# Weight chunks of the projections: eight buffers of two times 128 rows instead of four of four times 128

## The reference, cut to what matters

```python
# first block
h = rms_norm(x, norm1_g) @ w_in            # 2048 x 6176: q, k, v, gates (32 columns), ...
x = x + concat([gla(h), dilated_attention(h)]) @ w_out      # 2048 x 2048
x = x + peer_ffn(rms_norm(x, norm2_g))     # gathers rows of two tables of 16384 x 2048
# second block
p = rms_norm_2(x, mix_norm_g) @ w_in_2     # lru, mlstm (8 gate columns), moba inputs
x = x + concat([lru(p), mlstm(p), moba(p)]) @ w_out_2       # 2048 x 2048
x = x + memory_cross_attention(rms_norm_2(x, xa_norm_g), rms_norm_2(mem, mem_norm_g), wq, wkv, wo)
return rms_norm_2(x, final_norm_g)
```

## Time and profile before

| what | value |
|---|---|
| median of 3 runs | 2442.86 us |
| the profiled execution: its own time | 2440.96 us |
| its span in the trace | 2439.2 us |
| PE busy | 2017.3 us, 83% |
| DVE busy | 1354.1 us, 56% |
| ACT busy | 623.8 us, 26% |
| POOL busy | 630.3 us, 26% |
| mean granted TensorE clock | 0.948 |

### The profile page before, as it was taken

The page is one execution under the profiler, slowest core; times in us unless marked ns, Lnnn a source line. Parts: engine busy times, 40 slices in busy tenths (PEclk is TensorE's granted clock), DMA queues, the critical chain, the costliest instruction groups (busy, mean ns, idle before and its releaser), DMA issues. The chain is left out here.

```text
span 2439.2 us, 21677 instructions
## 1 busy us (share of the span) xinstructions
PE 2017.3 (83%) x8013; PEld 1331.2 (55%) x8013; DVE 1354.1 (56%) x1820; ACT 623.8 (26%) x901; POOL 630.3 (26%) x523
## 2 busy tenths in 40 slices
PE   6999867984988989777777888898771899999975
PEld 5888746873444444322233434443220888999874
DVE  4446537447554556455555654665547755555444
ACT  4334325321011111111111111011001554354333
POOL 0000000006543544445355434444533000000000
PEclk9999958996999999999999999999996899999988
DMA  5555501729999999999999999999998544465531
GB/s 197 197 195 190 199 1 47 264 85 382 421 422 422 422 421 422 423 421 419 421 422 420 416 422 421 416 420 423 421 422 343 180 160 158 146 205 186 188 122 70
DMA packets 102203, 727.64 MB, mean 298 GB/s; under 512 B 11840, under 2 KB 11968, under 8 KB 19808
## 3 DMA queue, kind: packets, MB, share of 16 engines
q0 software_dynamic: 73728, 536.90, 53.1%
q1 hardware_dynamic: 28384, 189.52, 22.0%
HBM read 722.18 MB, written 4.19 MB: 298 GB/s over the span
## 5 line engine op out<-in xcount | busy, mean ns | idle before, releaser
L1248 PE MATMUL bank<-ring,work 128*128 128x512 f32 x1920 | 894.0, 609 | 240.1 <-DMA ring<-in_peer_up_dram,work 238.7
L1492 DVE CUSTOM_DVE_ANT_0 ring<-ring,mix_t 128x2048 f32<-128x2048 f32 x256 | 584.2, 2291 | 526.7 <-DMA ring<-in_peer_down_dram,work 526.5
L1248 PEld LDWEIGHTS bank<-ring,work 128*128 128x128 f32 x1920 | 350.5, 192 | 716.5 <-issue 504.3
L449 DVE TENSOR_TENSOR ring_r<-ring,ring_r 128x2048 fp32r<-128x2048 f32 (+2 forms) x150 | 320.0, 2136 | 319.4 <-ACT ring_r L428 319.0
L1376 POOL DMA_INDIRECT ring<-in_peer_down_dram,work x256 | 316.6, 1237 | 440.1 <-DVE work L1449 238.2
L1385 POOL DMA_INDIRECT ring<-in_peer_up_dram,work x240 | 284.4, 1185 | 480.4 <-PE bank L1248 421.6
L482 PE MATMUL bank<-ring_r,mix_r 128*128 128x512 f32 (+1 forms) x1248 | 393.2, 386 | 0.0
L428 ACT ACTIVATE ring_r<-ring 128x2048 fp32r<-128x2048 f32 (+2 forms) x150 | 267.6, 1787 | 307.1 <-DMA ring<-in_w_out_dram 90.4
L482 PE MATMUL bank<-ring_r,act_r 128*128 128x512 f32 (+1 forms) x864 | 309.4, 388 | 12.6 <-DVE ring_r L449 12.6
L1316 ACT ACTIVATE work<-const,work 128x128 f32<-128x128 f32 x240 | 91.5, 399 | 734.3 <-PE bank L1248 733.1
L482 PEld LDWEIGHTS bank<-ring_r,mix_r 128*128 128x128 f32 x1248 | 233.6, 188 | 43.5
(11 more groups left out here) (354 smaller groups left out, 1336.3 us busy)
## 6 DMA issues: line engine op xcount, KB each, us to landing
ring<-in_w_out_dram SPq DMA_DIRECT2D x32, 1024.0 KB, 4.8
ring<-in_w_in_qk_dram SPq DMA_DIRECT2D x24, 1024.0 KB, 4.8
ring<-in_w_in_rest_dram SPq DMA_DIRECT2D x24, 1024.0 KB, 4.8
ring<-in_w_in_mo_dram SPq DMA_DIRECT2D x24, 768.0 KB, 4.4
h<-in_w_query_dram SPq DMA_DIRECT2D x8, 2048.0 KB, 10.4
ring<-in_w_in_ml_oz_dram SPq DMA_DIRECT2D x12, 1024.0 KB, 4.8
h<-in_xa_wkv_dram SPq DMA_DIRECT2D x4, 2048.0 KB, 16.8
ring<-in_w_in_lru_dram SPq DMA_DIRECT2D x8, 1024.0 KB, 4.9
```

What stands on the lines that cost most here:

```text
L449: dve.tensor_tensor(low(c), raw(c), plain(high(c)), ALU.subtract).then_inc(k.weights_low, 1)
L1248: m = pe.matmul(B[c][:, :], diag[:, j % DEPTH, :], up_row(j)[:, c * 512:(c + 1) * 512], start=first, stop=last)
L1492: dve.tensor_tensor_reduce(down_row(j), down_row(j), xn[:, t, :], 1.0, 0.0, ALU.mult, ALU.add, dots[:, p, j:j + 1]).then_inc(down_used, 1)
```

## The change

`DEEP` = 2 sets how many times 128 rows a chunk has; there are 16 / DEEP = 8 slots of half the size over the same memory, so the ring holds the same bytes. The two gate jobs take 8 times 128 rows, in two chunks each. A tick stays what it was in work: `PER_TICK` = 2 chunks. `AHEAD` stays at 3 ticks, which are now 6 chunks; the work beside the projections, the activation splits and the take-outs keep their places relative to the weights.

```diff
@@ class Program
+        self.pieces = shaped(self.ring[:, :], 2 * SLOTS, DEEP * 512)
+        self.pieces_r = shaped(self.ring_r[:, :], 2 * SLOTS, DEEP * 512)
@@
-SLOTS = 4
-AHEAD = SLOTS - 1
+DEEP = 2
+SLOTS = 16 // DEEP
+PER_TICK = 4 // DEEP
+AHEAD = 3
@@ class Job
-    def __init__(self, w, kind, dest, act, m=P, keep=None, add=False, deep=4):
+    def __init__(self, w, kind, dest, act, m=P, keep=None, add=False, deep=None):
-        self.deep, self.chunks = deep, KC // deep
+        self.deep = deep or DEEP
+        self.chunks = KC // self.deep
@@ def project
     def high(c):
-        return k.slots_r[:, SLOTS + c.slot, 0:c.job.deep * c.job.cols]
+        return k.pieces_r[:, SLOTS + c.slot, 0:c.job.deep * c.job.cols]
     def parts_at(p):
-        per_chunk = chunks[0].job.deep // 4
+        per_chunk = max(1, chunks[0].job.deep // 4)
+        if chunks[0].job.deep < 4:
+            return range(p // PER_TICK, p // PER_TICK + 1) if p % PER_TICK == 0 and p // PER_TICK < len(splits) else range(0)
         return range(len(splits))[p * per_chunk:(p + 1) * per_chunk]
     def taken_at(p):
-        return [chunks[p - AHEAD]] if 0 <= p - AHEAD < len(chunks) and chunks[p - AHEAD].completing else []
+        last = p - AHEAD * PER_TICK + PER_TICK - 1
+        return [chunks[last]] if 0 <= last < len(chunks) and chunks[last].completing else []
+    def at_tick(at, p):
+        if p % PER_TICK == 0:
+            at(p // PER_TICK)
@@ SP, ACT, DVE and PE programs
-                at(p - AHEAD)
+                at_tick(at, p - AHEAD * PER_TICK)
-                at(p)
+                at_tick(at, p)
@@ def build, def second_block
-        gates_job = Job(..., whole_act, m=GATE_M, keep=32, deep=KC)
+        gates_job = Job(..., from_act, m=GATE_M, keep=32, deep=KC // 2)
-            stream.chunks[stream.at(out2, e, s)].needs = needs
+            stream.chunks[stream.at(out2, e, s * PER_TICK)].needs = needs
```

More of the change, by code:

```diff
@@ L230, in __init__ @@
         self.groups = self.cols // m if kind == "feat" else NT
-        self.deep, self.chunks = deep, KC // deep
+        self.deep = deep or DEEP
+        self.chunks = KC // self.deep
         self.add_waits = ()
         if kind == "fold":
-            self.blocks, self.chunks = 4, 4 // deep
+            self.blocks, self.chunks = 4, 4 // self.deep
     def in_order(self):
@@ L302, in load @@
         at = deep * (c.b * c.job.chunks + c.s if c.job.kind == "fold" else c.s)
-        dst = shaped(self.k.slots[:, c.slot, 0:deep * c.job.cols], deep, c.job.cols)
+        dst = shaped(self.k.pieces[:, c.slot, 0:deep * c.job.cols], deep, c.job.cols)
         sp.dma_start(dst, src[:, at:at + deep, :]).then_inc(self.k.loaded[c.slot], 16)
@@ L356, in high @@
     def high(c):
-        return k.slots_r[:, SLOTS + c.slot, 0:c.job.deep * c.job.cols]
+        return k.pieces_r[:, SLOTS + c.slot, 0:c.job.deep * c.job.cols]
     def low(c):
-        return k.slots_r[:, c.slot, 0:c.job.deep * c.job.cols]
+        return k.pieces_r[:, c.slot, 0:c.job.deep * c.job.cols]
     def raw(c):
-        return k.slots[:, c.slot, 0:c.job.deep * c.job.cols]
+        return k.pieces[:, c.slot, 0:c.job.deep * c.job.cols]
     def parts_at(p):
-        per_chunk = chunks[0].job.deep // 4
+        per_chunk = max(1, chunks[0].job.deep // 4)
+        if chunks[0].job.deep < 4:
+            return range(p // PER_TICK, p // PER_TICK + 1) if p % PER_TICK == 0 and p // PER_TICK < len(splits) else range(0)
         return range(len(splits))[p * per_chunk:(p + 1) * per_chunk]
@@ L400, in _ @@
             for p in range(len(chunks)):
-                at(p - AHEAD)
+                at_tick(at, p - AHEAD * PER_TICK)
                 if p >= stream.started:
                     stream.load(sp, p)
-            rest(len(chunks) - AHEAD)
+            rest(len(chunks) // PER_TICK - AHEAD)
             if upcoming is not None:
@@ L416, in _ @@
             at, rest = beside.runner(act, beside.scalar)
-            for p in range(len(chunks) + AHEAD):
-                at(p - AHEAD)
+            for p in range(len(chunks) + AHEAD * PER_TICK):
+                at_tick(at, p - AHEAD * PER_TICK)
                 for n in parts_at(p)[:1]:
@@ L430, in _ @@
                     split_high(act, n)
-            rest(len(chunks))
+            rest(len(chunks) // PER_TICK)
         @block.vector
@@ L463, in _ @@
                 pe.wait_ge(k.weights_low, c.n + 1)
-                a_hi, a_lo = job.act(c.s)
+                a_hi, a_lo = job.act(c.s, job.deep)
                 w_hi, w_lo = shaped(high(c), job.deep, job.cols), shaped(low(c), job.deep, job.cols)
@@ L2372, in build @@
         beside = Beside()
-        rotate_beside(k, beside, in1.out(qk_job, qk_job.blocks - 1), in1.at(rest_job, 0))
+        rotate_beside(k, beside, in1.out(qk_job, qk_job.blocks - 1), in1.at(rest_job, 0) // PER_TICK)
         project(k, in1, "in1", split_act, upcoming=out1, beside=beside)
@@ L2399, in build @@
         k.recycle()
-        second_block(k, split_act, from_act, whole_act, residual)
+        second_block(k, split_act, from_act, residual)
         mem_q_job = Job(ins["xa_wq"], "feat", lambda b, g: k.h[:, g * T:(g + 1) * T], from_act)
@@ L2412, in build, with second_block @@
         last_norm(k)
-def second_block(k, split_act, from_act, whole_act, residual):
+def second_block(k, split_act, from_act, residual):
     ins = k.ins
@@ L2421, in second_block @@
     feat = lambda at: lambda b, g: k.h[:, at(b) + g * T:at(b) + (g + 1) * T]
-    gates = Job(ins["w_in_ml_gates"], "feat", lambda b, g: mem.gates_t, whole_act, m=GATE_M, keep=8, deep=KC)
+    gates = Job(ins["w_in_ml_gates"], "feat", lambda b, g: mem.gates_t, from_act, m=GATE_M, keep=8, deep=KC // 2)
     lru = Job(ins["w_in_lru"], "feat", feat(lambda b: (S_LRU_X, S_LRU_Z)[b]), from_act)
@@ L2427, in second_block, with mixed @@
     mo = Job(ins["w_in_mo"], "feat", feat(lambda b: (S_MO_Q, S_MO_K, S_MO_Z)[b % 3] + b // 3 * 3 * T), from_act)
-    def mixed(s):
-        at = slice(4 * s, 4 * s + 4)
+    def mixed(s, n):
+        at = slice(n * s, n * s + n)
         if at.start < 4:
```

3 lines of the change are left out of this document (1 added, 2 removed).

## The result

The changed kernel takes 2420.61 us (2418.28 to 2422.53, four runs) against 2442.24 (2438.48 to 2443.34, four runs) for the kernel before: a ratio of 0.9914, with a 95% interval of 0.9897 to 0.9931. The profiled executions took 2422.53 and 2440.96 us; their spans are 2420.7 and 2439.2, so the two traces, which all of the following compares, differ by 18.5 us and not by the full 21.6.

A forecast was written before the change was run, and what follows sets the result against it. PE was taken to bound the projections and transfers the expert stage, which keeps its time. Starts 6.3, gla's start 1.3 and in2's waits 4.0 sum to 11.6 us off 2442.86: 2431.3, say 2431.4 us, range 2425 to 2439.

The forecast's parts named there:

- Price of an instruction: ACT and DVE chunk splits: 150 more instructions each, 27 us on ACT, 22 on DVE, all taken as covered.
- the rival of the chunk borders: Projections: each of 150 new borders costs PE 0.15 us, giving 2453.8 us; chance 0.06 together with lost cover.
- Loads: Weight queue: twice the transfers cost nothing at share 0.58; its rival, loads become the bound, 2560 us, chance 0.02.
- Starts of projections: PE's first-chunk waits: 1.7 us saved at out1, mem_q, mem_out, 0.6 at in1 and in2; 6.3 us together.
- Clock: After each projection start: same falls to the low clock, the rise moving with the start, so 6.3 us is kept.
- The other case that the step named: Projection starts: if the clock's rise stayed in place, gained time runs at half speed, 3.2 us instead of 6.3.
- Start of `gla`: PE's 6.89 us wait on a small transfer behind in1's last load: 1.3 us saved, bounds 0 and 1.3.
- Waits inside in2: PE's waits on DVE or ACT within in2: 4.0 us saved, bounds 7.9 gained and 2.3 lost.
- the 7.9: In2: total of four kinds of PE wait on DVE or ACT, 3.0 + 2.1 + 1.6 + 1.2 us.
- The moba waits: In2: four PE waits, 3.0 us in all, each expected to shrink by 0.4 to 0.7 us.
- More than forecast: Rival: all 7.9 us of in2's waits go, and a clock fall with them; 2427.4 down to 2424 us, chance 0.07.

The follow-up runs named there:

- e4: Kernel before, with out1's fourth early 1 MB load issued behind gla's small transfers; median 5.5 us under the kernel before, eight runs, fastest 2428.65 us.
- e3: Changed kernel plus an unused 512 KB transfer queued ahead of gla's small ones; 9 us over the changed kernel by the two ratios.
- e6: Changed kernel plus an unused 768 KB transfer queued ahead of gla's small ones; two runs, median not given in the text.
- e7: Changed kernel plus an unused 1024 KB transfer queued ahead of gla's small ones; two runs, median not given in the text.
- e8: Changed kernel plus an unused 256 KB transfer queued ahead of gla's small ones; two runs, median not given in the text.
- e2: Changed kernel with loads still halved, but ACT and DVE taking two pieces in one instruction; 2431.78 us, ratio 0.997 to the kernel before.
- e1: Kernel before with whole loads, but ACT and DVE making each chunk in two instructions; 2430.94 us, ratio 0.9965 to the kernel before.

## Why the prediction was wrong, and where it was right

**Price of an instruction: right.** 1055 and 1221 ns against 1045 and 1220. The 150 more on each engine showed nowhere. In1 took 269.6 us from its first to its last matmul instead of 269.3, and the 0.3 more are the low clock at its start, which PE's work overlapped by 5.8 us instead of 5.2. Where that overlap is the same (3.4 us), in1 with the old chunks (e4) and with the 49 more of the new ones (e3, e6, e7, e8) takes the same 268.5 us, within 0.02. That is the answer to the rival of the chunk borders, which wanted 0.077 us for each.

**Loads: right.** A share of 0.65 instead of 0.58, and 0.68 with 256 KB, with PE busy throughout. Half the bytes land in 3.5 us rather than 4.8, so a smaller load takes longer for each byte. The rule of the Trainium skill, DMA: Bandwidth & Descriptors, Bandwidth, to batch transfers to 1 MiB or more, rests there on transfers issued from GpSimd. As a rival for this queue of SP the runs at 512 and 256 KB do not bear it out: a half load is issued every 2.7 us and lands after 3.5, so the loads overlap, and at a share of 0.65 or 0.68 the queue is not at its bound.

**Starts of projections: right in the waits, wrong in what is kept.** The waits shrank by 0.6, 1.7, 0.6, 1.7 and 1.7 us, 6.4 together where 6.3 were forecast. The spans kept 0.3, 0.7, 1.0, 0.9 and 0.5, together 3.4. This is the first step that failed, "Clock", as the prediction put it: "I expect the same falls, and the rise to move with the start." The rise did not move with it. At out1 both kernels have 6.8 us at the low clock, and PE works in 6.0 of them after and in 3.8 before (the third window above): the 2.2 us more of work there are done at half speed, which costs 1.1 of the 1.7 us gained. The other profiles bear it out: the clock rose 10.2 to 10.6 us after PE's last matmul ahead of out1 where the wait there was 6.6 us (before, e2, e4), and 9.5 to 10.7 us after it where the wait was 4.9 us or less (the other seven). The other case that the step named, 3.2 us in place of 6.3, is the one that came.

**Start of `gla`: a little over.** 0.8 us for 1.3. It lies between the prediction's two bounds, and the 5.6 us that it wanted for the wait were reached nowhere (5.7 at the least, in e2 and e4).

**Waits inside in2: mis-sized.** The prediction worked out 5.1 us by its chains and then took half of the 7.9, 4.0, on the ground that ACT's added time might eat into it. It didn't. Nor were the 7.9 us all: the view of the earlier trace rows has three more waits below those shown, 1.7 us together, which the prediction left out.

```profile
PE bank L1960 <- DVE work L1793: 0.7, 1, 0.7
PE bank L2216 <- ACT work L2272: 0.5, 1, 0.5
PE bank L2193 <- ACT h L390: 0.5, 1, 0.5
```

The first two are gone after the change. PE's idle time in in2 fell from 9.95 to 3.23 us (435.90 - 425.95 and 425.80 - 422.57, windows above), 6.7 us for the 4.0. The chains hold where they were worked out: L1951's wait by 0.7, L1969's wholly. The moba waits were put at 0.4 to 0.7 each of four and went wholly, 3.0 us. Beside the idle time, PE's busy time fell by 3.4 us with the same 2709 matmul rows. This is the clock again, here in favour of the changed kernel's profile. The kernel before has a low stretch in the midst of in2, behind the 2.1 us wait for L1951's step:

```profile
1945.70:1949.10 3.40, 3.40 (x19) 3.40 (x19) 1.16 (x2) 1.48 (x1) 0.00 (x0) 0.53 0.20 83
```

and the profile of the changed kernel, at the same place of the program, has none:

```profile
1938.80:1942.20 3.40, 3.40 (x30) 3.40 (x30) 2.98 (x7) 0.56 (x1) 0.00 (x0) 1.00 0.24 60
```

That is 1.7 us of work given back, and the low stretch at in2's start, which PE's work overlapped by 4.7 us before and by 3.4 after in the granted clock, gives some 0.6 more; 1.1 us I can't assign. But this is luck and not the change's doing. e3, e7 and e8 have the same code in in2 as the changed kernel, and their profiles have the low stretch in its midst (here e7), and 5.0 to 5.4 us of PE's work at the low level at its start:

```profile
1943.60:1947.00 3.40, 3.40 (x18) 3.40 (x17) 3.19 (x7) 0.84 (x1) 0.00 (x0) 0.50 0.02 5
```

e6, like the changed kernel, has none. With it PE worked for 424.9 to 425.2 us in in2 (e3, e7, e8), without it for 422.8 and 422.9 (e6 and the changed kernel), so about 2.4 of the 10.1 us are this luck and about 7.7 the change's (from the kernel before to e3, e7 and e8 the stage is 8.2 to 8.9 us shorter). e1 and e2, which give 5.5 and 1.9 us, 7.4 together, have the low stretch too. That leaves an us or so at most which only the two changes together would give.

**What no step had: `gla`.** This is the step that failed by most: the prediction read `gla` only up to its start and put the stage itself at nothing, without a reason. It gave 6.7 us, the largest single item of the miss. It has two durations by where its start falls against the clock, and I had not looked at its clock at all. The granted clock of 0.58 was to be had from one window of the trace of before, and would have said that a shift of its start could be worth several us either way. That a shift shortened it and did not lengthen it was luck; nothing in the prediction could have told which. The last rival, "More than forecast", had in2's waits gone and a fall of the clock saved. Most of the waits went, and the fall was missing in the profile, though not by the change; the time lies below its 2424 to 2427 too, since it lacks `gla`.

Set in terms of the sum, between the profiles: starts 3.4 for 6.3, `gla`'s start 0.8 for 1.3, in2 10.1 for 4.0, `gla` 6.7 for nothing, and 2.5 us lost in stages that the change doesn't touch: 18.5 for 11.6. Of the 2.5 the expert stage has 1.5, within what it varies by between profiles. The other 1.1 fit the low clock, at which PE worked for 1.0 us more in the dilated attention and for 1.2 us more in the normalisation. Without `gla`'s 6.7, in2's 2.4 and these 2.5 the change itself gave 11.9 us (3.4, 0.8 and 7.7), near the 11.6 of the sum, but only because two errors cancel: 3.4 for 6.3 at the starts and 7.7 for 4.0 in in2. The medians differ by 3.1 us more than the profiles; the changed kernel's four runs lie in two pairs, 2418.3 and 2419.0, 2422.3 and 2422.5, and the profiled one is in the upper pair.

## What to carry to other kernels

The latency of the first matmul of a stage is the whole chain load, split, multiply for one chunk, so a smaller chunk shortens it as long as the engines ahead have spare time; the price of a cut was 0.15 to 0.2 us an engine here (149 to 195 ns), and it is paid under cover until that engine becomes the bound. Read the granted clock of every stage that has waits in it before summing: of time saved in front of a matmul that runs at the low clock, about half is kept when the rise stays where it was (3.4 of 6.4 us here). And when the measured gain of a change is larger than its mechanism, look for a stage that it doesn't touch but shifts; here a third of the gain is that, and 512 KB more on a queue took it back in e3. And before a difference between two profiles is put down to a change, look at a third profile with the same code in that stage: here it showed that 2.4 us of in2's gain were chance.

## What was not expected of the hardware

`gla`, with the same instructions, took 54.3 to 55.2 us or 61.6 to 62.1 us, by where its start fell against the clock. The windows of its low stretches: in the kernel before

```profile
324.40:334.60 10.20, 5.98 (x63) 5.29 (x64) 7.96 (x20) 2.83 (x7) 0.00 (x0) 0.51 0.00 0
...
341.50:367.10 25.60, 16.64 (x75) 12.14 (x76) 5.30 (x14) 4.86 (x20) 0.00 (x0) 0.50 0.00 0
```

and in the changed kernel

```profile
324.50:331.30 6.80, 3.19 (x51) 2.87 (x52) 5.00 (x10) 1.15 (x2) 0.00 (x0) 0.52 0.00 1
331.30:351.80 20.50, 14.49 (x127) 11.44 (x125) 5.70 (x18) 8.18 (x24) 0.00 (x0) 0.99 0.00 1
351.80:359.40 7.60, 2.50 (x10) 1.73 (x11) 5.05 (x13) 1.19 (x2) 0.00 (x0) 0.50 0.00 0
```

PE began `gla` 1.1 us earlier in the changed kernel, at 303.97 instead of 305.04. In both the clock falls at about 324.2, which is 20.3 us after the start in the one and 19.1 in the other. The changed kernel is back at the full level (0.99) at about 331 and keeps it until 351.5; the one before is back at 334.4, falls again at 341.2 (0.50) and stays at the low level to the end of the stage. So a microsecond of shift against the clock goes with 0.72 or 0.58 over the stage. It is not a matter of more or less delay: e7, at 21.8 us, has the long duration again, with a granted clock of 0.61. Why the stretches behind the fall come out so isn't shown.
